# Values of two pairs of heads multiplied together by products of 256 columns

## The reference

```python
def swa_sink_attention(hn, w_q, sinks, w_o, k, v):
    nc = S // CHUNK                       # 8 chunks of 64 tokens
    q = (hn @ w_q).reshape(B, nc, CHUNK, N_KV_HEADS, GROUP, HEAD_DIM)
    kw = window_blocks(k..., nc)          # keys of the chunk before and of its own
    vw = window_blocks(v..., nc)
    s = einsum('bcqkgd,bcwkd->bckgqw', q, kw) * (HEAD_DIM ** -0.5)
    s = where(valid, s + alibi, NEG_INF)
    m = maximum(max(s, axis=-1, keepdims=True), sink)
    p = exp(s - m)
    p = p / (sum(p, axis=-1, keepdims=True) + exp(sink - m))
    o = einsum('bckgqw,bcwkd->bcqkgd', p, vw)
    return o.reshape(B, S, N_Q_HEADS * HEAD_DIM) @ w_o
```

## Time and profile before

| | |
|---|---|
| median of 3 runs | 1099.47 us (1099.43 to 1099.68) |
| time of the profiled execution | 1100.99 us |
| span of the profiled execution | 1099.1 us |
| TensorE matmuls busy (PE) | 1087.9 us, 99% of the span |
| VectorE busy (DVE) | 789.5 us, 72% |
| ScalarE busy (ACT) | 564.0 us, 51% |
| granted TensorE clock, mean | 0.999 |

### The profile page before, as it was taken

One profiled execution on the slowest core, in us unless ns is written; L12 is line 12 of the kernel. 1 busy time (PEld: TensorE's weight loads), 2 busy tenths in 40 slices (PEclk: granted clock), 3 DMA queues, 4 the chain that ended last, 5 costly groups with the idle time before them and its releaser, 6 DMA issues.

```text
span 1099.1 us, 17600 instructions
## 1 busy us (share of the span) xinstructions
PE 1087.9 (99%) x6973; PEld 978.1 (89%) x6973; DVE 789.5 (72%) x1131; ACT 564.0 (51%) x997; POOL 27.0 (2%) x40
## 2 busy tenths in 40 slices
PE   8999999999999999999999999999999999999998
PEld 7887787889999999988888888889999999998886
DVE  5878985788888888853457698468988888863334
ACT  6377474565455555542235676555455555542223
POOL 2000000000000000001221000000000000000000
PEclk9999999999999999999999999999999999999999
DMA  6332233232333234344541201132333333342311
GB/s 205 96 107 69 77 107 115 96 96 78 97 115 115 85 110 116 114 140 130 158 105 62 60 1 39 39 115 62 93 97 116 116 89 104 115 143 102 97 43 77
DMA packets 150964, 107.25 MB, mean 98 GB/s; under 512 B 23921, under 2 KB 140769, under 8 KB 150882
## 3 DMA queue, kind: packets, MB, share of 16 engines
q1 hardware_dynamic: 150882, 106.12, 32.2%
HBM read 104.01 MB, written 2.10 MB: 97 GB/s over the span
## 4 chain that ended last, share of the span: by engine, by line
PE 97%; ACT 1%; DVE 1%; issue 1%; DMA 0%; DVEq 0%; SPq 0%; ACTq 0%
PE ps L1823 11%; PE ps L1827 11%; PE ps L1825 11%; PE ps L1596 11%; PE ps L1597 11%; PE ps L1600 11%; PE ps L1576 9%; PE ps L1578 8%; PE ps L1577 8%; PE ps L1754 1%; PE ps L1928 1%; PE ps L1606 1%; PE ps L1955 1%; PE ps L1982 1%; PE ps L1980 1%
## 5 line engine op out<-in xcount | busy, mean ns | idle before, releaser
L1047 DVE TENSOR_TENSOR w_lo<-raw,w_hi 128x1024 fp32r<-128x1024 f32 x97 | 121.5, 1255 | 164.4 <-ACT w_hi L625 164.2
L625 ACT CAST w_hi<-raw 128x1024 fp32r<-128x1024 f32 x98 | 102.1, 1046 | 166.0 <-PE ps L1600 147.5
L1823 PE MATMUL ps<-t_hi,w_hi 128*128 128x256 f32 x608 | 172.4, 284 | 0.6 <-ACT u L864 0.6
L1825 PE MATMUL ps<-t_lo,w_hi 128*128 128x256 f32 x608 | 172.3, 283 | 0.0
L1827 PE MATMUL ps<-t_hi,w_lo 128*128 128x256 f32 x608 | 172.2, 283 | 0.0
L1576 PE MATMUL ps<-x_hi,w_hi 128*128 128x512 f32 (+1 forms) x392 | 140.8, 359 | 0.6 <-DVE x_lo L1077 0.6
L1577 PE MATMUL ps<-x_lo,w_hi 128*128 128x512 f32 (+1 forms) x392 | 138.1, 352 | 0.0
L1578 PE MATMUL ps<-x_hi,w_lo 128*128 128x512 f32 (+1 forms) x392 | 138.1, 352 | 0.0
L1596 PE MATMUL ps<-w_hi,t_hi 128*128 128x512 f32 x352 | 137.3, 390 | 0.0
L1597 PE MATMUL ps<-w_lo,t_hi 128*128 128x512 f32 x352 | 137.1, 390 | 0.0
L1827 PE MATMUL ps<-x_hi,w_lo 128*128 128x256 f32 x456 | 129.2, 283 | 0.0
(11 more groups left out here) (223 smaller groups left out, 2195.6 us busy)
## 6 DMA issues: line engine op xcount, KB each, us to landing
raw<-in_ffn_w_gu SPq DMA_DIRECT2D x88, 512.0 KB, 4.7
raw<-in_ffn_w_down SPq DMA_DIRECT2D x44, 512.0 KB, 3.3
raw<-in_a_w_in SPq DMA_DIRECT2D x24, 512.0 KB, 4.0
raw<-in_a_w_out SPq DMA_DIRECT2D x12, 512.0 KB, 3.4
raw<-in_b_w_o SPq DMA_DIRECT2D x16, 256.0 KB, 4.0
raw_q<-in_b_w_q SPq DMA_DIRECT2D x12, 256.0 KB, 4.6
h<-in_x SPq DMA_DIRECT2D x4, 512.0 KB, 5.5
result<-h SPq DMA_DIRECT2D x3, 512.0 KB, 2.6
```

The costliest lines, as they stand in the source:

```text
L625: nc.scalar.copy(halves(t)[0], raw_of(t)).then_inc(w_hi_ready, 1)
L1047: v.tensor_tensor(lo, raw_of(t), hi.bitcast(F32), ALU.subtract).then_inc(w_lo_ready, 1)
L1823: nc.tensor.matmul(ps[:, b, 0:HS], w_hi[:, slot, cols], hi, start=start, stop=False, skip_group_check=True)
L1825: nc.tensor.matmul(ps[:, b, 0:HS], w_hi[:, slot, cols], lo, start=False, stop=False, skip_group_check=True)
```

## The change

Values of the pairs 0 and 1, 2 and 3, 4 and 5 are multiplied together by `values_two(m)`, m even. The probabilities of two pairs lie side by side (`p_hi` and `p_lo` get an index m % 2; `p_hi` lies now where `work` is), so that one window takes two query chunks of both pairs, 256 columns. Its output goes into two banks, 0 and 3 (`two_outputs`), half of the tokens in each. Windows that would cross the banks are cut in two. `values_two` has 6 windows of 256 columns and 3 of 128, so 27 products for two pairs. It stands at odd m behind the second part of the queries; at even m TensorE has no values, and all eight windows of the queries stand ahead of `turn_p(m)`. `turn_p` of an even m waits in addition until bank 0 is read (`olo_ready` at m). `o_high_two` and `o_low_two` stand where `o_high(m-1)` and `o_low(m-1)` stood for m = 2, 4, 6, with two copies each of the size of one before; the order on ScalarE and VectorE is otherwise kept. Pairs 6 and 7 have their own values as before.

In the feed-forward parts, `keep_p1_p6(0)` now stands ahead of `s_high(1)`, in the first of the 19 steps only.

```diff
-    p_hi = sb("p_hi", [P, 2, TC, P], F32R)
-    p_lo = sb("p_lo", [P, 2, TC, P], F32R)
+    p_lo = sb("p_lo", [P, 2, 2 * TC, 2, CHUNK], F32R)
...
+    p_hi = sb("p_hi", [P, 2, 2 * TC, 2, CHUNK], F32R, at["work"])
...
+        def two_outputs(half):
+            return bank([0, 3][half]).rearrange("p (m n) -> p m n", m=2)
...
-                    s_high(c + 1)
-                    keep_p1_p6(c)
+                    if c == 0:
+                        keep_p1_p6(c)
+                        s_high(c + 1)
+                    else:
+                        s_high(c + 1)
+                        keep_p1_p6(c)
...
+            def o_high_two(m):
+                for half in range(2):
+                    act.wait_ge(o_ready, m + 1 + half)
+                    nc.scalar.copy(o_hi[:, m:m + 2, HS * half:HS * half + HS], two_outputs(half)).then_inc(ohi_ready, 1)
...
-                if m >= 1:
+                if m in (2, 4, 6):
+                    o_high_two(m - 2)
+                elif m == PAIRS_H - 1:
                     o_high(m - 1)
...
+            def o_low_two(m):
+                for half in range(2):
+                    dve.wait_ge(ohi_ready, m + 1 + half)
+                    cols = slice(HS * half, HS * half + HS)
+                    v.tensor_tensor(o_lo[:, m:m + 2, cols], two_outputs(half), o_hi[:, m:m + 2, cols].bitcast(F32),
+                                    ALU.subtract).then_inc(olo_ready, 1)
...
                 if m > 0:
                     pe.wait_ge(plo_ready, 2 * m)
+                    if m % 2 == 0:
+                        pe.wait_ge(olo_ready, m)
...
+            def window(into, c, part, start, stop):
+                odd = c % 2
+                at = (slice(None), odd) + part
+                nc.tensor.matmul(into, v_hi[:, c, :], p_hi[at], start=start, stop=False, skip_group_check=True)
+                nc.tensor.matmul(into, v_hi[:, c, :], p_lo[at], start=False, stop=False, skip_group_check=True)
+                return nc.tensor.matmul(into, v_lo[:, c, :], p_hi[at], start=False, stop=stop, skip_group_check=True)
...
+            def values_two(m):
+                if m > 0:
+                    pe.wait_ge(olo_ready, m)
+                def chunks(c, first, n):
+                    half, col = (c + first) // TC, (c + first) % TC
+                    into = two_outputs(half).rearrange("p m (c n) -> p c m n", n=CHUNK)[:, col:col + n, :, :]
+                    k = 2 * (c // 2) + first
+                    return window(into, c, (slice(k, k + n),), c in (0, TC), bool(c % 2))
+                pe.wait_ge(plo_ready, 2 * (m + 1) + 1)
+                for c in range(0, 2 * TC, 2):
+                    chunks(c, 0, 2)
+                pe.wait_ge(plo_ready, 2 * (m + 1) + 2)
+                chunks(1, 0, 2)
+                chunks(3, 0, 1).then_inc(o_ready, 1)
+                chunks(3, 1, 1)
+                chunks(5, 0, 2)
+                chunks(7, 0, 1).then_inc(o_ready, 1)
...
-            queries(2, range(2, DC - 1))
+            queries(2, range(2, DC))
             turn_p(0)
-            queries(2, range(DC - 1, DC))
-            values(0)
             for m in range(1, PAIRS_H - 2):
                 scores(m + 1)
-                queries(m + 2, range(0, 5))
-                turn_p(m)
-                queries(m + 2, range(5, DC))
-                values(m)
+                if m % 2 == 1:
+                    queries(m + 2, range(0, 5))
+                    turn_p(m)
+                    queries(m + 2, range(5, DC))
+                    values_two(m - 1)
+                else:
+                    queries(m + 2, range(0, DC))
+                    turn_p(m)
```

More of the change, by code:

```diff
@@ L976, in p_high @@
                 act.wait_ge(pt_ready, 2 * m + odd + 1)
-                n = 4 * P - odd * CHUNK
-                nc.scalar.copy(p_hi[:, odd, :, :].rearrange("p c n -> p (c n)")[:, 0:n], ps[:, odd, 0:n])\
-                    .then_inc(phi_ready, 1)
+                n = 2 * TC - odd
+                src = ps[:, odd, 0:n * CHUNK].rearrange("p (c n) -> p c n", n=CHUNK)
+                nc.scalar.copy(p_hi[:, odd, 0:n, m % 2, :], src).then_inc(phi_ready, 1)
             def o_high(m):
@@ L1499, in p_low @@
                 dve.wait_ge(phi_ready, 2 * m + odd + 1)
[L1500 to L1503, removed]
+                n = 2 * TC - odd
+                src = ps[:, odd, 0:n * CHUNK].rearrange("p (c n) -> p c n", n=CHUNK)
+                v.tensor_tensor(p_lo[:, odd, 0:n, m % 2, :], src, p_hi[:, odd, 0:n, m % 2, :].bitcast(F32),
+                                ALU.subtract).then_inc(plo_ready, 1)
             def o_low(m):
@@ L1524, in _ @@
                 divided(m)
-                if m >= 1:
+                if m in (2, 4, 6):
+                    o_low_two(m - 2)
+                elif m == PAIRS_H - 1:
                     o_low(m - 1)
@@ L1966, in turn_p @@
                 ins.then_inc(pt_ready, 1)
+            def window(into, c, part, start, stop):
[4 more added lines that the diff above has]
+                return nc.tensor.matmul(into, v_lo[:, c, :], p_hi[at], start=False, stop=stop, skip_group_check=True)
             def values(m):
-                if m > 0:
-                    pe.wait_ge(olo_ready, m)
+                pe.wait_ge(olo_ready, m)
                 for odd in range(2):
@@ L1975, in values @@
                         c = 2 * i + odd
[L1976 to L1983, removed]
-                ins.then_inc(o_ready, 1)
+                        n = min(2, 2 * TC - c)
+                        into = ps[:, 3, c * CHUNK:(c + n) * CHUNK].rearrange("p (c n) -> p c n", n=CHUNK)
+                        ins = window(into, c, (slice(2 * i, 2 * i + n), m % 2), c == 0, bool(odd))
+                ins.then_inc(o_ready, 1)
+            def values_two(m):
+                if m > 0:
+                    pe.wait_ge(olo_ready, m)
+                def chunks(c, first, n):
[12 more added lines that the diff above has]
+                chunks(7, 0, 1).then_inc(o_ready, 1)
             def o_rows(k, t, halves=(0, 1)):
```

## The result

The changed kernel takes 1109.45 us in the median (1106.89 to 1111.29, 4 runs) beside 1099.58 us for the kernel before on the same chip: ratio 1.0081, 95% interval 1.0069 to 1.0094, so it is slower. The forecast was 1101.7 us with a range to 1105.0. The sign was right, the size was not, and the range missed the time.

The account below looks back on a forecast made before the run. TensorE, busy 99% of the span, was taken to bound the kernel. Attention at +3.1 us and feed-forward at -0.94 us summed to +2.2 us, from 1099.47 to 1101.7 us, with a range of 1100.2 to 1105.0.

Parts of the forecast that it names:

- The chain of 5.1 us: Even turns: scores wait on ScalarE and VectorE until 5.1 us after the transposes start, so TensorE waits 3.8 us.
- the turns of 12.5, 12.3 and 11.8 us: Attention turns: 12.5 us for turn 1, 12.3 for even m = 2, 4, 11.8 for odd m = 3, 5, against 11.33.
- the wait ahead of the first `values_two`: Turn 1: TensorE has its queries done and waits 0.7 us for `p_low(1,0)`.
- the transposes of m = 6: End of the loop: they wait for `o_low_two(4)` and start some 2.3 us after `scores(7)`, before 2.19.
- The wide products: Values of two pairs: 256-column products 0.12 us apart save 2.18 us for each two pairs, 6.5 us for three.
- rival C: New access patterns cost: 0.04 us on 54 products, 0.1 on 12 copies, +3.4, 1105 us at the far end; chance 0.05.
- Rival B: Even turns: the saving holds and scores do not wait for `q_low`; 1091.5 us; chance 0.06.
- the sum: Whole kernel: +3.1 us in attention less 0.94 in feed-forward, +2.2 us, median 1101.7 us.
- the end of the loop: Attention's last turns: `turn_p(6)` waits for both halves of `o_low_two(4)`, costing +0.1 us.
- the feed-forward part: `keep_p1_p6(0)` ahead of `s_high(1)` removes a 0.47 us wait for copy `u` in two places, -0.94 us.
- rival A: TensorE's clock falls in the two long waits, 1.3 us each, +2.7, 1104.4 us; one of them, 1103.0; chance 0.22.
- the wait of the first pair: Ahead of `scores(2)`: TensorE waits 2.3 us for `q_low(2)`; pairs 0 and 1 together give 0.0.

Follow-up runs that it names:

- kernel with filled waits: Changed kernel plus unread 512-column products behind turn_p(0) (9) and turn_p(2), turn_p(4) (16 each); 1101.96 us, ratio 1.0014 to the kernel before.
- second measurement: Kernel before with only keep_p1_p6(0) ahead of s_high(1), measured again with more rounds; 1099.85 us, ratio 0.9992.
- `fill(5)`: Changed kernel plus 5 extra products of 512 columns behind turn_p(2) and turn_p(4); 1109.60 us, ratio 1.0088 to the kernel before.
- the other: Changed kernel measured again without further change, in another execution; 1110.45 us, ratio 1.0092 to the kernel before.
- cut queries: Changed kernel with one query window behind turn_p(0), three behind turn_p(2) and turn_p(4); 1099.69 us, ratio 0.9992, and again 1099.31 us, ratio 0.9988.
- the kernel with the queries moved ahead: Changed kernel with q_high(m+2) ahead of p_high(m) and q_low(m+2) ahead of p_low(m) for m = 0, 2, 4; 1100.90 us, ratio 1.0002.

## Why the prediction was right and wrong

**Right: the waits and their cover.** The chain of 5.1 us from the transposes to `q_low` (5.10 after), the turns of 12.5, 12.3 and 11.8 us (12.50, 12.32, and 11.82 where the clock is full), the wait ahead of the first `values_two` (0.44 of idle time, 0.7 expected), the transposes of m = 6 at 2.45 us behind the scores (2.3 expected). The wide products:

```profile
641.79 0.28 PE L2000 MATMUL ps<-p_lo,v_hi 128*128 128x256 f32 x1
...
643.34 0.28 PE L2001 MATMUL ps<-p_hi,v_lo 128*128 128x256 f32 x1
```

are 1.55 / 13 = 0.12 us apart, so that part of rival C, a price for writing in runs of 64 columns, is out. Its other part, slower copies, is out as well: the median of `p_high` is 0.56 us and that of `p_low` 0.65 in both kernels, `o_high` takes 0.57 (0.59 before) and `o_low` 0.68 (0.67). Rival B, no waits, is out by the list of waits. The kernel with filled waits is the one that the sum described: +3.4 us in the attention (3.1 forecast; the end of the loop cost 0.26 instead of 0.1), and 1.0014 (1.0005 to 1.0024) as its ratio where the forecast was 1.0020.

**Right: the feed-forward part.** -0.94 was forecast. The ratio of the second measurement gives -0.9 us, with an interval that reaches +0.1, so by itself it does not tell the gain from none; the traces give 0.54 and 0.58 us for the two places (0.47 each forecast).

**Wrong: the clock, twice.** The step that failed is in rival A. I gave it 0.22, with the argument that "nothing shows that 3.7 us are enough", and so the forecast went on as if TensorE would come back from each wait at full speed. In every profile of these kernels it came back at 1.2 GHz after a wait of 3.7 us (five of five), and after the ones of 2.4 us of `fill(5)` as well (two of two). The second part is its price. I took a stretch of 3.13 us from the start of the kernel and came to 1.3 us a wait. Measured are 2.1 and 2.6 us in the profiled execution of the result, 3.1 and 3.2 in the other, because the lower level lasted 6.8 us each time, at most a third of it inside the wait, and the wait of the first pair, which I left out of the price, cost another 0.9 us in two of four profiles. With +2.2 for the sum and 4.7 to 7.1 for the clock the forecast would have been 1106.4 to 1108.8 from a median of 1099.5. The runs lie at 1106.9 to 1111.3; up to 1.9 us of the rest can be the start, below. That the change would lose was right for its own reason (the filled kernel loses too), but more than half of the measured loss is the clock, which the forecast put at nothing.

The Trainium skill, page "TensorE: Matmul & The Clock Gate", section "HAM oscillation — how this bites in real kernels", warns of gaps between bursts of matmuls, and this case bears its warning out: 3.7 us of waiting, 1.2 GHz behind it. The waits of 1.4 to 2.4 us behind which the clock fell here are shorter than the gaps that the section describes, and there the measurement decides. For the two waits of 3.7 us the section would have been a better guide than the absence of such a wait in the trace.

**The wide products saved what was forecast, and it was spent.** 6.5 us of TensorE's work were removed. The values had stood behind the transposes, where they hid the way from the transposes through ScalarE and VectorE to the next scores. In even turns that cover is gone.

**Open.** What sets the moment at which the clock falls, inside the wait in one execution and at its end in another, was not tried, and neither was why a wait of 2.2 us costs the clock in two of four profiles. Waits were filled only to two degrees: 5 products left 2.4 us of waiting and the clock fell, 16 left none and it stayed.

## What to carry to other kernels

Before removing work from the bound engine, ask what that work was covering: take the time from its last producer to its next consumer on the other engines, and subtract what is still left to run in between. A wait on TensorE costs its length and then the clock: here 2.1 to 3.2 us on top of each wait of 2.4 to 3.7 us, and shorter waits cost it in some executions. If a wait can't be avoided, put other work of the same engine into it; even useless products were worth 4.6 to 7 us here.

## What the hardware showed that was not expected

**Useless work made the kernel faster.** 41 extra products of 512 columns, some 9.4 us of TensorE's time at 0.23 each, took the attention from 100.43 us (102.91 in the other execution) to 95.85 us.

**Short waits can cost the clock too.** Of the six waits for `q_low` of 1.4 to 1.8 us in the two profiles with cut queries, the clock fell behind one, and it fell behind the wait of 1.6 us in the kernel with the queries moved ahead. In both it fell 1.7 to 2.0 us after the wait had ended, with TensorE at work between. That these waits are the reason is argued from their being the last pause ahead of the fall; neither was filled to test it.

**Two starts.** The first product of 256 columns takes 0.55 us in some executions and 0.35 in others, whatever the kernel: in the first the products are 0.21 us apart until 15 to 17 us, in the second 0.12 from the beginning. The column of the granted clock reads 1.00 over both starts, so that this is 1.2 and 2.4 GHz is inferred from the distances: where the column reads 0.50, products of 512 columns are 0.43 us apart instead of 0.23, the same doubling. The kernel with the feed-forward part alone has a span of 1098.3 us with the first start and 1096.4 with the second; the line is the first product of that second execution:

```profile
11.59 0.36 PE L1580 MATMUL ps<-x_hi,w_hi 128*128 128x256 f32 x1 [0.95 <-DVE x_lo L1081]
```

These 1.9 us are a good part of the spread that the kernel before shows from run to run, 1099.3 to 1103.5. They fit its profiled execution, which had the first start and took 1.5 us more than the median, and with them a difference of 1 us is hard to tell even with ten runs.
